# Layer norm ahead of a turn in one pass, scale and shift applied to the transposed result, projections interleaved with the turn

## The reference

```python
for i in range(DEPTH):                                    # DEPTH = 2
    y = hybrid_mixer(x, w_in[i], ..., w_out[i], i, cos, sin)   # projections, four kinds of attention, projection
    x = layer_norm(ALPHA * x + y, ln1_g[i], ln1_b[i])
    y = peer_ffn(x, peer_wq[i], peer_keys[i], peer_u[i], peer_v[i])
    x = layer_norm(ALPHA * x + y, ln2_g[i], ln2_b[i])
# layer_norm: (x - mean) * rsqrt(var + eps) * g + b, over the 2048 columns
```

## Time and profile before

| | |
|---|---|
| time, median of 3 runs | 4208.52 us |
| profiled execution, span | 4207.5 us (its own time is taken as this span and the 1.0 us by which the median exceeds it) |
| PE busy, matmul | 4081.4 us, 97% |
| DVE busy | 2589.3 us, 62% |
| ACT busy | 1908.7 us, 45% |
| POOL busy | 499.9 us, 12% |
| mean DMA rate | 193 GB/s |

### The profile page before, as it was taken

One profiled execution on the slowest core, in us unless ns is written; L12 is line 12 of the kernel. 1 busy time (PEld: TensorE's weight loads), 2 busy tenths in 40 slices (PEclk: granted clock), 3 DMA queues, 4 the chain that ended last, 5 costly groups with the idle time before them and its releaser, 6 DMA issues. The chain is left out here.

```text
span 4207.5 us, 73345 instructions
## 1 busy us (share of the span) xinstructions
PE 4081.4 (97%) x24964; PEld 3660.6 (87%) x24964; DVE 2589.3 (62%) x5020; ACT 1908.7 (45%) x2568; POOL 499.9 (12%) x728
## 2 busy tenths in 40 slices
PE   8999899999999999999899998999999999999997
PEld 7877799999999888888678777999999998888886
DVE  5655558656855555555656655586578555555556
ACT  4444344554455444444344443445544554444443
POOL 0100000341044000000001000003410440000000
PEclk9977999999999999999999679999999999999999
DMA  5512445557755666666445124555586456666664
GB/s 219 190 61 91 179 172 208 183 178 241 233 180 185 218 226 249 231 226 229 175 174 187 49 103 177 181 203 180 179 251 224 177 187 217 232 249 227 231 229 176
DMA packets 243065, 810.94 MB, mean 193 GB/s; under 512 B 24320, under 2 KB 157440, under 8 KB 157440
## 3 DMA queue, kind: packets, MB, share of 16 engines
q1 hardware_dynamic: 206080, 775.78, 52.4%
q10 hardware_dynamic: 36864, 33.57, 2.3%
HBM read 756.82 MB, written 52.43 MB: 192 GB/s over the span
## 5 line engine op out<-in xcount | busy, mean ns | idle before, releaser
L908 DVE TENSOR_TENSOR lo<-raw,hi 128x1024 fp32r<-128x1024 f32 x1312 | 1639.6, 1251 | 1455.1 <-ACT hi L632 1421.0
L632 ACT ACTIVATE hi<-raw 128x1024 fp32r<-128x1024 f32 x1312 | 1390.3, 1060 | 1582.0 <-PE bank L590 759.1
L537 PE MATMUL bank<-xh,hi 128*128 128x256 f32 x4096 | 1172.1, 286 | 1.4 <-ACT scr L743 1.4
L539 PE MATMUL bank<-xh,lo 128*128 128x256 f32 x4096 | 1161.0, 283 | 0.0
L538 PE MATMUL bank<-xl,hi 128*128 128x256 f32 x4096 | 1160.8, 283 | 0.0
L588 PE MATMUL bank<-hi,xh 128*128 128x512 f32 x2048 | 798.3, 390 | 1.3 <-ACT gelu_out L752 0.9
L590 PE MATMUL bank<-hi,xl 128*128 128x512 f32 x2048 | 797.8, 390 | 0.0
L589 PE MATMUL bank<-lo,xh 128*128 128x512 f32 x2048 | 797.7, 390 | 0.0
L537 PEld LDWEIGHTS bank<-xh,hi 128*128 128x128 f32 x4096 | 787.2, 192 | 1.8 <-ACT scr L743 1.8
L538 PEld LDWEIGHTS bank<-xl,hi 128*128 128x128 f32 x4096 | 787.5, 192 | 0.0
L539 PEld LDWEIGHTS bank<-xh,lo 128*128 128x128 f32 x4096 | 786.8, 192 | 0.0
(11 more groups left out here) (136 smaller groups left out, 3470.2 us busy)
## 6 DMA issues: line engine op xcount, KB each, us to landing
raw<-u_t SPq DMA_DIRECT2D x256, 1024.0 KB, 4.8
raw<-v_t SPq DMA_DIRECT2D x256, 1024.0 KB, 4.8
raw<-w_in SPq DMA_DIRECT2D x84, 1024.0 KB, 4.8
raw<-w_out SPq DMA_DIRECT2D x32, 1024.0 KB, 4.8
raw<-wq SPq DMA_DIRECT2D x32, 1024.0 KB, 4.8
gelu_scratch<-gelu_out ACTq DMA_DIRECT2D x256, 128.0 KB, 2.2
scr<-gelu_scratch SPq DMA_DIRECT2D x256, 128.0 KB, 4.6
gates_scratch<-arena SPq DMA_DIRECT2D x32, 512.0 KB, 9.8
```

The costliest lines, as they stand in the source:

```text
L537: pe.matmul(h, wh, xh[:, c, :], start=(c == 0), stop=False)
L539: last = pe.matmul(h, wl, xh[:, c, :], start=False, stop=(c == DC - 1))
L632: act.activation(hi[j % NSPLIT][:], half, ACT.Copy).then_inc(hi_done, 1)
L908: dve.tensor_tensor(lo[j % NSPLIT][:], half, hi[j % NSPLIT][:].bitcast(F32), ALU.subtract).then_inc(lo_done, 1)
```

## The change

Ahead of a turn the layer norm only subtracts the mean and multiplies by the inverse deviation, in one pass for each 128 x 512 piece, six by ACT and two by DVE. The transposed result has the columns on the partitions, so scale and shift are two values for each partition there (`cols_1`, `cols_2`, by DMA): `turn_high` becomes two activations of 256 columns with scale and bias, and `turn_low` two tensor_scalar operations of 256 columns into `turn_f` and a subtraction of 512 columns. The residual `x` gets its scale and shift later from POOL (`affine`, 8 multiplications and 8 additions of 128 x 512), once the whole turn is done: `affine(0)` stands ahead of POOL's rotary additions in the input projection, `affine(1)` ahead of its routing work. The first layer has g = 1 and b = 0 there, set by POOL at the start. For the output, DVE applies scale and shift after the loop, and the output leaves in eight DMAs.

All three turns are interleaved with the eight halves of the first group behind them (`turned_for`). The last four halves of the output projection's last group are done for token block 0, then for block 1, and the norm of block 0 starts between. The last y banks are closed one at a time. An extra Sqrt on ACT, whose result isn't used, stands behind turn 1 and ahead of the `v_t` halves. The diff, cut to its core:

```diff
+@block.gpsimd
+def _(pool):
+    pool.memset(ln_gb[:, 0, :], 1.0)
+    pool.memset(ln_gb[:, 1, :], 0.0)
+    pool.memset(cols_2[:, 0, :], 1.0)
+    pool.memset(cols_2[:, 1, :], 0.0)
 with nc.Fori(0, DEPTH) as layer:
 def of_layer(t):
...
-        def turn(r, src):
-            for k in range(DC // 2):
-                n = r * (DC // 2) + k
-                if n >= 4:
-                    pe.wait_ge(turn_lo, n - 3)
-                if r == 2 and k % 2 == 0:
-                    q = k // 2
-                    pe.wait_ge(ln_done, q + 1)
-                    if q < 2:
-                        pe.wait_ge(ln_done_pool, q + 1)
-                    else:
-                        pe.wait_ge(ln_done_last, q - 1)
-                for c in (2 * k, 2 * k + 1):
-                    for b in range(NB):
-                        last = pe.transpose(bank[4 + k % 4][:, (c % 2) * L + b * P:(c % 2) * L + (b + 1) * P],
-                                            src[:, b, c * P:(c + 1) * P], ident[:])
-                last.then_inc(turned, 1)
-        def tokens_by_half(n, j, kc, banks, first_c, last_c, width=W):
+        def turn_step(r, src, k):
+            n = r * (DC // 2) + k
+            if n >= 4:
+                pe.wait_ge(turn_lo, n - 3)
+            if r == 2 and k % 4 == 0:
+                pe.wait_ge(normed_act, D // W + k // 4 + 1)
+            elif r == 2 and k % 2 == 0:
+                pe.wait_ge(normed_dve, k // 4 + 1)
+            for c in (2 * k, 2 * k + 1):
+                for b in range(NB):
+                    last = pe.transpose(bank[4 + k % 4][:, (c % 2) * L + b * P:(c % 2) * L + (b + 1) * P],
+                                        src[:, b, c * P:(c + 1) * P], ident[:])
+            last.then_inc(turned, 1)
+        def turned_for(r, src, kc):
+            for k in range(2 * kc, min(2 * kc + 2, DC // 2)):
+                turn_step(r, src, k)
+            pe.wait_ge(turn_lo, r * (DC // 2) + kc + 1)
+        def tokens_by_half(n, j, kc, banks, first_c, last_c, width=W, blocks=range(NB), release=True):
...
             if free:
                 pe.wait_ge(rope_evac, g * NB - NB)
             for kc in range(HPG):
+                if first:
+                    turned_for(0, x, kc)
                 tokens_by_half(g * HPG + (AT_IN + kc), kc, kc, banks, 0, DC - 1, width)
                 if prev is not None and kc in (2, 3):
                     turn_rope(prev, kc - 2)
-        turn(0, x)
-        pe.wait_ge(turn_lo, 8)
-        in_group(0, 0, None, free=False)
+        in_group(0, 0, None, free=False, first=True)
         in_group(1, 1, 0, free=False)
...
         pe.wait_ge(mixed_done, 1)
-        turn(1, mixed)
-        pe.wait_ge(turn_lo, 16)
+        def out_half(g, kc, **only):
+            return tokens_by_half(AT_OUT + g * HPG + kc, kc, kc, [bank[2 * (g % 2)], bank[2 * (g % 2) + 1]], 0, DC - 1,
+                                  **only)
         for g in range(D // W):
             if g >= 2:
                 pe.wait_ge(out_evac, NB * (g - 1))
-            for kc in range(HPG):
-                tokens_by_half(AT_OUT + g * HPG + kc, kc, kc, [bank[2 * (g % 2)], bank[2 * (g % 2) + 1]], 0, DC - 1)
-        turn(2, x)
-        pe.wait_ge(turn_lo, 24)
+            for kc in range(HPG - NSPLIT if g == D // W - 1 else HPG):
+                if g == 0:
+                    turned_for(1, mixed, kc)
+                out_half(g, kc)
+        for kc in range(HPG - NSPLIT, HPG):
+            last = out_half(D // W - 1, kc, blocks=(0,), release=False)
+        last.then_inc(b0_done, 1)
+        for kc in range(HPG - NSPLIT, HPG):
+            out_half(D // W - 1, kc, blocks=(1,))
         for g in range(D // W):
             if g >= 2:
                 pe.wait_ge(q_stored, 4 * (g - 1))
             for kc in range(HPG):
+                if g == 0:
+                    turned_for(2, x, kc)
...
         for b in range(NB):
-            for j in range(BODY - 4, BODY):
-                pe.wait_ge(lo_done, N_HALVES - BODY + j + 1)
-                pe.wait_ge(al_done, NT - NRAW + j // 2 + 1)
-                last = products(b, j, j // 2 % 2, stop=j >= BODY - 2)
-                if j >= BODY - 2:
-                    last.then_inc(y_done, 1)
+            for q in range(D // W):
+                for j in (BODY - 4 + q // 2, BODY - 2 + q // 2):
+                    pe.wait_ge(lo_done, N_HALVES - BODY + j + 1)
+                    pe.wait_ge(al_done, NT - NRAW + j // 2 + 1)
+                    last = products(b, j, j // 2 % 2, stop=j >= BODY - 2, qs=(q % 2,))
+                last.then_inc(y_done, 1)
...
-        def turn_high(r):
-            for k in range(DC // 2):
-                act.wait_ge(turned, r * (DC // 2) + k + 1)
-                act.activation(xh[:, 2 * k:2 * k + 2, :].rearrange("p a b -> p (a b)"), bank[4 + k % 4][:],
+        def turn_high(r, k):
+            act.wait_ge(turned, r * (DC // 2) + k + 1)
+            if r == 1:
+                act.activation(xh[:, 2 * k:2 * k + 2, :], bank[4 + k % 4][:].rearrange("p (a b) -> p a b", a=2),
                                ACT.Copy).then_inc(turn_hi, 1)
+                return
+            cols = cols_1 if r else cols_2
+            for c in (2 * k, 2 * k + 1):
+                last = act.activation(xh[:, c, :], bank[4 + k % 4][:, c % 2 * L:(c % 2 + 1) * L], ACT.Identity,
+                                      bias=cols[:, 1, c:c + 1], scale=cols[:, 0, c:c + 1])
+            last.then_inc(turn_hi, 1)
...
-        turn_high(0)
-        for j in range(NSPLIT):
-            split_hi(AT_IN, 0, j, first=True)
+        for k in range(DC // 2):
+            if k < NSPLIT:
+                split_hi(AT_IN, 0, k, first=True)
+            turn_high(0, k)
...
                 split_hi(AT_OUT, 0, SPLIT_UNITS.index(u))
-        turn_high(1)
+        for k in range(DC // 2):
+            turn_high(1, k)
+        act.activation(small[:, 48:49], lay_b[:, 2:3], ACT.Sqrt)
         for m in range(NSPLIT, N_OUT):
...
-        def layer_norm(k):
-            for b in range(NB):
-                act.wait_ge(ln_var, k * NB + b + 1)
-                act.activation(norm[:, b, 2:3], norm[:, b, 1:2], ACT.Sqrt, bias=lay_b[:, 2:3]).then_inc(ln_root, 1)
-            act.wait_ge(ln_factors, k + 1)
-            for q in range(2):
-                cols = x[:, 1, q * W:(q + 1) * W]
-                act.activation(cols, cols, ACT.Identity, bias=norm[:, 1, 4:5], scale=norm[:, 1, 3:4]).then_inc(ln_normed, 1)
-        layer_norm(0)
-        turn_high(2)
+        def root(k, b):
+            act.wait_ge(ln_var, k * NB + b + 1)
+            act.activation(norm[:, b, 2:3], norm[:, b, 1:2], ACT.Sqrt, bias=lay_b[:, 2:3]).then_inc(ln_root, 1)
+        def normalize(k, b, qs):
+            act.wait_ge(ln_factors, k * NB + b + 1)
+            for q in qs:
+                cols = x[:, b, q * W:(q + 1) * W]
+                act.activation(cols, cols, ACT.Identity, bias=norm[:, b, 4:5], scale=norm[:, b, 3:4]).then_inc(normed_act, 1)
+        split_hi(AT_WQ, 0, 0)
+        root(0, 0)
+        split_hi(AT_WQ, 0, 1)
+        normalize(0, 0, range(D // W))
+        root(0, 1)
+        normalize(0, 1, (0, 2))
+        act.wait_ge(cols_in, 16)
+        turn_high(2, 0)
+        split_hi(AT_WQ, 0, 2)
+        turn_high(2, 1)
+        split_hi(AT_WQ, 0, 3)
+        for k in range(2, DC // 2):
+            turn_high(2, k)
         for m in range(NSPLIT, N_WQ):
             split_hi(AT_WQ, m // BODY, m % BODY)
...
+        act.activation(small[:, 48:49], lay_b[:, 2:3], ACT.Sqrt)
         with act.Fori(0, N_V // BODY - 1) as i:
             for j in range(BODY):
                 second_body(i, j)
         for j in range(BODY):
             second_body(N_V // BODY - 1, j, last=True)
-        layer_norm(1)
+        root(1, 0)
+        normalize(1, 0, range(D // W))
+        root(1, 1)
+        normalize(1, 1, (0, 2))
...
+        def affine(k):
+            pool.wait_ge(turn_lo, k * DC + DC // 2)
+            if k:
+                pool.wait_ge(ln_in, 16)
+            for n in range(NB * D // W + 1):
+                if n < NB * D // W:
+                    q, b = n // NB, n % NB
+                    cols = x[:, b, q * W:(q + 1) * W]
+                    pool.tensor_tensor(cols, cols, ln_gb[:, 0, q * W:(q + 1) * W], ALU.mult).then_inc(ln_scaled, 1)
+                if n:
+                    q, b = (n - 1) // NB, (n - 1) % NB
+                    cols = x[:, b, q * W:(q + 1) * W]
+                    pool.wait_ge(ln_scaled, NB * D // W * k + n)
+                    pool.tensor_tensor(cols, cols, ln_gb[:, 1, q * W:(q + 1) * W], ALU.add).then_inc(residual_ready, 1)
+        affine(0)
         for g in range(8):
             for b in range(NB):
...
+        pool.wait_ge(ln_in, 32)
+        pool.wait_ge(cols_in, 32)
...
-        def turn_low(r):
-            for k in range(DC // 2):
-                dve.wait_ge(turn_hi, r * (DC // 2) + k + 1)
-                two = slice(2 * k, 2 * k + 2)
```

(106 more changed lines are left out.)

65 lines of the change are left out of this document (21 added, 44 removed).

## The result

Changed kernel 4219.51 us median (4215.96 to 4222.6, 12 runs); before, on the same chip, 4209.52 (4207.90 to 4212.98, 12 runs). Ratio 1.0024, 95% interval 1.0016 to 1.0033: slower by about 10 us, just over the 0.2% that can be told from no change. The forecast was 4215.6, 7.1 above the 4208.52 of the kernel before. The profiled execution has a span of 4215.5 against 4207.5, so 8.0 of the 10 can be read from the two traces.

What follows compares the result with a forecast made beforehand. PE, busy 97% of the span, was taken as the bound, so only its standing still could move. 31.6 + 2.6 - 17.4 - 15.6 + 5.9 = +7.1 on 4207.5 gives 4214.6, median 4215.6; range 4193 to 4231.

Steps and rivals of the forecast that it cites:

- input stages, with the clock behind the stall: Input stages: PE waits for the rotary sum behind POOL's burst, then restarts at low clock; cost 16.2 and 15.4, together 31.6.
- turn 1: Turn 1: 5.1 lost against 3.8 before; cost 1.3 a layer, 2.6 in both, bounds -1 and +3 each.
- layer norm 1 and turn 2: Between output and query projection: 19.0 lost before, 10.4 after; gain 8.6 to 8.7 a layer, 17.4 in both.
- layer norm 2: Between a layer's last value products and the norm's end: end moves from 2103.50 to 2095.7; gain 7.8 a layer, 15.6.
- end: After the last norm: DVE's sixteen scale and shift operations and the last DMA take 14.1 instead of 8.2; cost 5.9.
- Z: Input stage: whole turn done at T+22.1, T being the first transpose; POOL's burst starts there and ends at Z+30.8.
- my case: Whole kernel: main forecast, POOL's burst stretched by the splits makes PE wait; sum +7.1, 4206 to 4226, chance 0.58.
- rival 1: Input stages: POOL is done in time, a split costing it under 0.1; clock 1.7 after half 4's pause; 4195.6, chance 0.22.
- sign of being wrong: Input stages: no wait of PE on POOL, or single POOL operations of 1.29 beside the splits.
- its larger half: Turn 1: 2.0 lost ahead of half 4, as hi(4) waits on ACT behind turns 6, 7 and the Sqrt's 1.28 table load.
- Rival 3: Layer norms: gain smaller because low clock lasts or `turn_low` is 2.1; 4223 to 4225, chance 0.08.
- Rival 2: Input stages: POOL slower on `x`, 0.35 an operation its own, burst 5.6 longer in each layer; 4226.8, chance 0.12.

Runs made afterwards that it cites:

- the kernel with the late Sqrt: Changed kernel with ACT's extra Sqrt and its table load moved from behind turn 1 to behind the output projection's split 8: 4217.23 us, ratio 1.0017 against before.
- The memory sets: Changed kernel with POOL's sixteen residual operations in the input stage replaced by sixteen memory sets, each as long as one operation alone: 4199.65 us, ratio 0.9973 against before.
- The kernel with the edit of layer norm 2: Changed kernel with block 0's last value products half by half again and its factors made behind block 1's first bank: 4209.08 us, ratio 0.9999 against before.

## Why the prediction held, term by term

| term, both layers | predicted | measured |
|---|---|---|
| input stages, with the clock behind the stall | 31.6 | 33.1 |
| turn 1 | 2.6 | 2.6 |
| layer norm 1 and turn 2 | -17.4 | -19.4 |
| layer norm 2 | -15.6 | -13.4 |
| end | 5.9 | 5.6 |
| start | 0 | -0.2 |
| sum | 7.1 | 8.3 (8.0 by the spans; the rest is drift in the long stages) |

**Input stages.** The chain was as predicted: Z (the end of the turn), then sixteen operations with eleven splits between them, then the sum, then PE. Z came at T+23.6 in layer 0 instead of 22.9 (22.1 + the 0.8 for that layer), the burst took 30.7, predicted 30.8, and the stall was 7.95 and 7.78 instead of 9.7. The pause ahead of half 4 was 4.3 instead of 4.9, and 1.05 of it comes from the splits that meet the burst's start. Behind that pause PE ran at half clock for 4.7 us, which my case left out (its own rival 1 had 1.7 for it):

```profile
38.00:39.00 1.00, 1.00 (x4) 0.50 0.06 16
...
42.00:43.00 1.00, 1.00 (x5) 0.93 0.97 410
```

That is 2.3 lost on seven halves, so PE came to the sums later and stood still for 7.95 instead of 9.7. It changes nothing in the sum, since POOL's chain decides when the sum is there: a shorter stall behind a slower approach. Mis-sized was the clock behind the stall: 2.0 a layer in the sum, and 3.6 in layer 0 (17.4 - 13.8) and 1.1 in layer 1 (17.9 - 16.8). By the windows alone the half clock costs 3.0 in layer 0 and 1.5 in layer 1. It is a spread rather than a size. In layer 0 of this execution the windows show half clock from the restart at 66.85 to 72.9, 6.0 us; in the kernel with the late Sqrt, whose first stage is the same and which restarts at 67.31, the clock is back by 70.2:

```profile
70.00:71.00 1.00, 1.00 (x6) 0.90 0.00 0
```

Its turn 1 comes 1.8 earlier (382.61) although its restart is 0.5 later; 1.5 of these 2.2 are the shorter half clock. In layer 1 it falls behind again: its first transpose is 2.7 earlier than in the changed kernel (2108.34), its turn 1 0.4 later (2481.07). So the same stall costs more or less from one execution to the next. The median of the changed kernel lies 4.0 above its profiled span, before 2.0 above, and these 2 us of the 10 no trace shows; that this spread is their cause is a guess.

**The contention.** One operation of POOL on 512 columns takes 1.29 alone and 2.25 to 2.28 behind a split, 0.97 more, against 0.98 from the earlier trace rows. The memory sets cost neither side anything. The rotary products, for which the prediction had no row beside POOL, take 0.68 and 0.41 beside the burst (at 54.02 and 54.62), as elsewhere (means of 0.68 and 0.41): they cost nothing. The prediction's sign of being wrong, "single POOL operations of 1.29 beside the splits", was put badly: such operations are there (51.72), and it is the next one that pays. By the Trainium skill ("SBUF — State Buffer", Who interferes with whom) a DVE instruction with two SBUF inputs contends with a GpSimd one that reads SBUF and not with one that only writes; both halves of this the two kernels show (2.23 a split beside the burst, 1.2 beside the sets). The Trainium skill's rule that whichever of the two starts first has the ports for the whole instruction and the other is fully blocked ("SBUF — State Buffer", SBUF: two separate sides) agrees with the order in the rows; by my sum it would have made the price 1.15 a split, and the measurement says 0.97. That this sum, about 4219, lies nearer to the measured 4219.51 than the forecast is chance, since the burst took 30.7 us and not 32.7.

**Turn 1.** Right in its sum, 1.4 and 1.2 (predicted 1.3 each). The late Sqrt confirms its larger half: without the table load ahead of `hi` 4, the wait there loses 1.5.

**Layer norm 1.** Gain 9.5 and 9.9 instead of 8.7. The first gap is 3.46 (predicted 3.4), the second 2.56 (2.2). The clock behind them is back at 492.7, 5.0 us at half clock and so 2.5 lost (2.5). The loss ahead of half 4, put at 1.2, was 1.03; that ahead of half 6, put at 1.1 for POOL's burst beside the splits, doesn't occur, and this is most of the difference. Rival 3 falls with it: the norm gained more, not less, and a `turn_low` takes 1.00 + 0.69 (L974, L978), not 2.1. Rival 2 falls by POOL's addition at 51.72, which takes 1.29 on `x` with `ln_gb`.

**Layer norm 2.** This is the step of the prediction that failed in part: gain 6.6 and 6.75 instead of 7.8. "With the banks closed one at a time only 3 instead of 12 matmuls stand ahead of that wait, so 45 are left: 2087.8" takes 45 matmuls at the full clock. The wait became 2.22, and PE's windows behind it are at 0.50:

```profile
2086.00:2087.00 1.00, 0.44 (x2) 0.86 0.00 0
2087.00:2088.00 1.00, 1.00 (x4) 0.50 0.79 139
...
2089.00:2090.00 1.00, 1.00 (x4) 0.50 1.02 426
```

The last product starts 11.65 after the wait (2098.21 - 2086.56) instead of 44 x 0.227 = 10.0: 1.7 lost to some 3.5 us at half clock. From the last product to the end of the norm it took 7.3 instead of 7.9, which gives back 0.6 of it; together that is the 1.1 by which the gain is short. The kernel with the edit of layer norm 2 has the wait at 0.18 and granted clock 1.00 in the same place, and its gap from there to the next transposes is shorter: 2084.65 to 2104.93, against 2086.56 to 2111.06. These 4.2 a layer are 2.0 for the nine matmuls that stand ahead of the wait again, 1.7 of the clock, and 0.5 for all the rest, the earlier factors among it; the median gains 10 in two layers.

**End.** 5.6 against 5.9. The sixteen operations ran from 4203.27 to 4213.0, 9.7 (predicted 9.8); the last DMA had 2.5 to go (4215.5 - 4213.0), against 2.6. DVE began 1.6 after ACT's end (1.5). These add up to 13.8; the prediction's own terms add up to 13.9, not to the 14.1 that it took, and that slip is most of the 0.3.

**Luck.** The mechanism of every large term held, but the closeness of the sum is in part luck: the misses are +1.5 in the input stages, -2.0 in layer norm 1, +2.2 in layer norm 2, -0.3 at the end and -0.2 at the start, and only together do they come to 1.2. The forecast was also put on a base of 4208.52, where twelve runs gave 4209.52.

What is shown: that the order on POOL makes the wait, and that reads beside the splits stretch the burst. What is only argued: that the untraced 2 us are the clock's spread.

## What to carry to other kernels

- Before work is given to an idle engine, look at what already stands in its queue behind the new work, and at when that is due: POOL was busy 12% of the span, and still the rotary sums had no room behind sixteen operations whose result nobody read for some 350 us (the burst ends at 65.5, its first reader on DVE, L1214, comes at 417.67).
- Where POOL and DVE get in each other's way, as POOL's operations and DVE's splits do here, their times have to be summed, not overlaid. Cost a burst by its duration alone plus what each neighbour that falls into it adds; here 19.9 + 11 x 0.98.
- A pause of PE is often dearer than its length: behind pauses of 2.2 to 8 us PE mostly ran 3 to 6 us at half clock, which cost another 1.5 to 3. Count it as a range from 0 to 3 us, not as one number.

## What was not expected of the hardware

A wait of 2.22 us in a stage in which PE is otherwise never idle was enough for the granted clock to fall to 0.50 for some 3.5 us. But a longer one can pass without it. The kernels without the burst, with memory sets and with the burst on DVE have the same pause ahead of half 4 in both layers, 3.23 to 3.25 us. Behind it PE ran at half clock for 0 and 6.2 us in the first of them (layer 0 and 1), 6.0 and 2.9 in the second, 2.9 and 6.0 in the third. These are the windows of PE in the first, just behind the pause in layer 0 and in layer 1:

```profile
36.00:37.00 1.00, 0.77 (x3) 1.00 0.00 0
...
2121.00:2122.00 1.00, 1.00 (x3) 0.50 0.00 0
```

Up to 3 us a pause thus depend on something that no row here names.

And in layer 0 the profile's granted clock and the matmuls disagree: between 17 and 22 us the windows list 1.00 while the matmuls follow each other every 0.43 us, as at 1.2 GHz; from 22 on every 0.23. In layer 1, at the same place, spacing and record agree on the low clock.

```profile
18.00:19.00 1.00, 1.00 (x4) 1.00 0.97 401
...
2116.00:2117.00 1.00, 1.00 (x4) 0.50 0.32 103
```

At the start of this program the spacing of the matmuls is what to go by.
